# Query split of the next attention group, on VectorE, moved from one block of a group to three

## What is computed

```python
q = (_rmsnorm(cq, q_norm_g) @ w_uq).reshape(B, S, MLA_HEADS, MLA_NOPE_DIM + MLA_ROPE_DIM)
q = jnp.concatenate([q[..., :MLA_NOPE_DIM], _rope(q[..., MLA_NOPE_DIM:], cos, sin)], axis=-1)
...
def one(qblk):                       # 128 queries of every head against all 2048 keys
    s = jnp.einsum('bqhd,bkhd->bhqk', qblk, k, preferred_element_type=jnp.float32) * scale
    p = jax.nn.softmax(s, axis=-1).astype(v.dtype)
    return jnp.einsum('bhqk,bkhd->bqhd', p, v)
```

## Time and profile before

| | |
|---|---|
| median of 3 runs | 2358.72 us (2356.21 to 2360.28) |
| profiled execution | 2355.62 us |
| its span in the trace | 2353.8 us |
| attention (754.3 to 1377.0 us of the span), PE busy | 600.29 of 622.70 us |
| the same stretch, DVE, ACT, POOL busy | 462.20, 365.57, 203.97 us |
| granted TensorE clock there | 1.00 of full speed (2.4 GHz) |

### The profile page before, as it was taken

One profiled execution on the slowest core, in us unless ns is written; L12 is line 12 of the kernel. 1 busy time (PEld: TensorE's weight loads), 2 busy tenths in 40 slices (PEclk: granted clock), 3 DMA queues, 4 the chain that ended last, 5 costly groups with the idle time before them and its releaser, 6 DMA issues. The chain is left out here.

```text
span 2353.8 us, 34599 instructions
## 1 busy us (share of the span) xinstructions
PE 2256.6 (96%) x11426; PEld 1894.3 (80%) x11426; DVE 1404.0 (60%) x2146; ACT 1156.8 (49%) x2160; POOL 1025.7 (44%) x762
## 2 busy tenths in 40 slices
PE   5999998999998999999999989998999999999998
PEld 4888887989897778777777768887888888877886
DVE  7333336444445777767677751215999999983342
ACT  4555534222324655555555545556556565653432
POOL 6322222222223432323333132332989999982454
PEclk9999999999999999999999999999999999999999
DMA  7533323434343533434342224331111211253653
GB/s 298 179 134 134 134 76 139 152 127 151 127 145 118 150 105 98 107 94 116 85 119 82 90 104 143 118 123 42 44 59 41 68 54 43 74 177 114 174 161 107
DMA packets 196117, 271.15 MB, mean 115 GB/s; under 512 B 10532, under 2 KB 137764, under 8 KB 191398
## 3 DMA queue, kind: packets, MB, share of 16 engines
q1 hardware_dynamic: 191398, 261.43, 34.7%
q10 hardware_dynamic: 4608, 8.39, 1.0%
HBM read 183.27 MB, written 86.51 MB: 115 GB/s over the span
## 5 line engine op out<-in xcount | busy, mean ns | idle before, releaser
L2353 POOL TENSOR_TENSOR conv_g<-conv_g,product 128x1024 f32<-128x1024 f32 x160 | 384.9, 2408 | 34.3 <-ACT product L2402 24.6
L2500 DVE SCALAR_TENSOR_TENSOR ps_b<-u,cols,ps_b 128x1024 f32<-128x1024 f32 x304 | 391.7, 1288 | 9.2
L2616 PE MATMUL ps_a<-ho_hi,wp_lo 128*128 128x512 f32 x768 | 300.8, 392 | 6.8 <-DVE h_left L2556 6.8
L2617 PE MATMUL ps_a<-h_left,wp_hi 128*128 128x512 f32 x768 | 300.0, 391 | 0.0
L2618 PE MATMUL ps_a<-ho_hi,wp_hi 128*128 128x512 f32 x768 | 299.9, 391 | 0.0
L2402 ACT ACTIVATE product<-u,cols 128x1024 f32<-128x1024 f32 x160 | 183.3, 1151 | 170.0 <-POOL conv_g L2353 168.7
L1605 ACT ACTIVATE pt_hi<-ps_pt 128x512 fp32r<-128x512 f32 x256 | 154.4, 604 | 197.5 <-PE ps_pt L1801 197.3
L1716 DVE TENSOR_TENSOR pt_lo<-ps_pt,pt_hi 128x512 fp32r<-128x512 f32 x256 | 175.9, 688 | 119.7 <-ACT pt_hi L1605 116.9
L1660 POOL TENSOR_TENSOR v_lo<-v_st,v_hi 128x512 fp32r<-128x512 f32 x64 | 84.2, 1316 | 237.0 <-DVE v_hi L1692 237.0
L1706 DVE TENSOR_REDUCE mx<-ps_s 128x1 f32<-128x512 f32 x248 | 167.0, 684 | 21.3 <-PE ps_s L1793 20.3
L2616 PEld LDWEIGHTS ps_a<-ho_hi,wp_lo 128*128 128x128 f32 x768 | 145.0, 189 | 38.6 <-DVE h_left L2556 8.7
(11 more groups left out here) (449 smaller groups left out, 5629.0 us busy)
## 6 DMA issues: line engine op xcount, KB each, us to landing
scratch_ret_pack<-pack SPq DMA_DIRECT2D x14, 1280.0 KB, 5.4
pack<-scratch_ret_pack SPq DMA_DIRECT2D x14, 1280.0 KB, 7.0
k_st<-scratch_k_t SPq DMA_DIRECT2D x64, 256.0 KB, 3.5
v_st<-scratch_v SPq DMA_DIRECT2D x64, 256.0 KB, 3.7
ada<-in_ada_w_dram SPq DMA_DIRECT2D x16, 768.0 KB, 6.2
wp_raw<-in_od_w_in_dram SPq DMA_DIRECT2D x24, 512.0 KB, 4.1
xt<-in_x_dram SPq DMA_DIRECT2D x16, 512.0 KB, 6.1
ada<-in_ada_w_dram SPq DMA_DIRECT2D x8, 1024.0 KB, 8.8
```

The source lines that it names most:

```text
L2353: pool.tensor_tensor(half(conv_g, h), half(conv_g, h), product[adds(c, i, h) % 2][:], ALU.add).then_inc(added, 1)
L2500: dve.scalar_tensor_tensor(acc[h], units(c, k, h), params(c, k), acc[h], ALU.mult, ALU.add).then_inc(tap, 1)
L2616: pe.matmul(dst, lo[:, k, :], h_hi[:, k, t], start=k == 0, stop=False)
L2617: pe.matmul(dst, hi[:, k, :], h_lo[:, k, t], start=False, stop=False)
```

## The change

The three DVE instructions of `split_q` become three functions. `rot_high` (cast of `q_rot`, with its waits for the query load and for the group before) now stands at the end of block 0, `query_high` (cast of `q_hi`) at the end of block 1, `rot_low` (the low rotary half) at the end of block 2, each behind that block's `v_hi`. Nothing is added or removed on any engine.

```diff
-            def split_q(m, sl):
+            def rot_high(m, sl):
                 hold(dve, st, q_in, 48 * (m + 1))
                 if not (isinstance(m, int) and m < 2):
                     hold(dve, st, s_done, 16 * (m - 1))
                 dve.tensor_copy(q_rot[sl][:], qr_st[:]).then_inc(rot_hi, 1)
+
+            def query_high(m, sl):
                 dve.tensor_copy(q_hi[sl][:], q_st[:]).then_inc(qhi_done, 1)
+
+            def rot_low(m, sl):
                 hold(dve, st, rot_hi, m + 1)
                 dve.tensor_tensor(q_rot[sl][ROPE:P, :], qr_st[ROPE:P, :], q_rot[sl][ROPE:P, :].bitcast(F32),
                                   ALU.subtract).then_inc(rot_ready, 1)
...
-                    if score and not last(n, 1) and b == 1:
-                        split_q(n + 1, 1 - s)
+                    if score and not last(n, 1) and b < 3:
+                        (rot_high, query_high, rot_low)[b](n + 1, 1 - s)
```

## The result

The changed kernel took 2366.99 us (median of 7 runs, 2362.34 to 2373.38) beside 2359.08 for the kernel before on the same chip (2356.21 to 2360.56). The ratio is 1.0036, 95% interval 1.0021 to 1.0050: about 8 us slower, where 7 us faster had been forecast. Its profiled execution took 2366.68 us, span 2364.9, that is 11.1 us more span than before. Two executions took far longer than all others of their kernels (8030.22 us, one of 32 of the kernel before beside experiments 1 to 4, and 3648.95 us, one of six of experiment 6); the ratios leave them out.

A forecast was written before the change was run, and what follows sets the result against it. PE was taken as the bound, waiting for DVE in block 2. Block 2 -12.1, block 3 +3.4 and step 0 +1.9 gave -6.8 us, 2351.9 for the median; the range was to take in 2346.5 and 2357.5 but not 2366.2.

The forecast's parts named there:

- What bounds: PE busy 96%; in block 2 it waits for the left-over tile's `pt_lo`, held by DVE's list, not ACT.
- block 2: PE's wait at its second turn, steps 1 to 14, vanishes: 12.1 us gained.
- `q_hi` at 0.42: The cast of `q_hi`, moved ahead of POOL's `v_lo` in block 1, takes about 0.42 us instead of 1.50.
- `rot_high` in block 0 free: Its 0.42 us behind `v_hi` is hidden by DVE's 0.70 us idle before block 1: cost 0.
- Step 0: `rot_high` waits for the first query load ahead of block 1's maxima; PE restarts 1.9 us later in step 1.
- Block 3: `rot_low` in block 2 delays block 3's bias by 0.60 us, so the next step's scores wait: 3.4 us in sum.
- Four more are in block 0 of a new pass of the loop, which no edit touches: Four of PE's 20 low-part waits, in block 0 of a new loop pass, taken as unaffected.
- it goes 0.6 us later with some 10 us in hand: SP's query load, now waiting for `rot_low` at the end of block 2, goes 0.6 us later at no cost.
- The rivals: Block 3's delay misses PE: 2349.0, chance 0.20; POOL first: 2366.2, 0.08; gain falls short: 2358.0, 0.17.
- rival 2: In block 2 POOL's `v_lo` starts first, `rot_low` costs 1.08 us more: +7.5 us, 2366.2; chance 0.08.

The follow-up runs named there:

- experiment 1: The changed kernel, but in step 0 the three instructions stay together in block 1 as before: 2363.09 us (ratio 1.0016).
- experiment 2: The changed kernel, but `rot_low` goes to block 1 behind `query_high`: 2356.36 us (ratio 0.9988).
- experiment 3: The changed kernel, but SP issues the 768 KB modulation load in block 1 instead of block 0: 2356.21 us (ratio 0.9989).
- experiment 4: The kernel before, with only the modulation load moved from block 0 to block 1: 2357.77 us (ratio 0.9994).
- experiment 6: The changed kernel with step 0 split as before and the modulation load issued in block 1: 2350.60 us (ratio 0.9959).
- experiment 7: The kernel before with `split_q` whole in block 1 ahead of the `v_hi` cast, and the modulation load in block 1: 2344.01 us (ratio 0.9932).
- experiment 8: The changed kernel with `rot_low` in block 0 behind `rot_high`, step 0 as before, modulation load in block 1: 2344.55 us (ratio 0.9935).
- experiment 11: The kernel before with `split_q` whole in block 1 ahead of the `v_hi` cast, modulation load where it was: 2347.91 us (ratio 0.9948).
- experiment 5: The kernel before, but SP also waits for block 3's multiply-add before the query loads, DVE's list untouched: 2366.70 us (ratio 1.0033).

## Why the prediction was wrong
- **What bounds, and block 2: right.** PE was held by DVE's list behind `split_q`; the wait is gone, 12.4 us for 12.1. (Step 1 had been put at 0.57 from its wait; cut like the others it is 0.48.)
- **`q_hi` at 0.42: right** (412 to 420 ns in all 15), and by the port, as experiment 2 shows for its neighbour.
- **`rot_high` in block 0 free: right** in all steps but 0.
- **Step 0: mechanism right, size off.** PE's restart was forecast 1.9 us later; it came 3.5 us later, and 1.6 us of lower clock followed, which the forecast had no term for and which came in other traces without the edit too. The chain was right as far as the wait for the load (4.8 forecast, 4.73), but it priced the subtraction at 0.69, not at POOL-first's 1.78, and the multiply at 1.01.
- **Block 3: mechanism right, size off.** 3.4 forecast, 4.9 in the trace. In the even steps PE waits 0.38 to 0.40 (0.31 forecast), in the odd ones 0.24 (0.04). From the start of `v_hi` to that of the gates it is now 0.45 + 0.72 = 1.17 us for 0.34, a shift of 0.83; I took 0.60 of a range that ended at 0.72.
- **The step that failed: "Four more are in block 0 of a new pass of the loop, which no edit touches", and "it goes 0.6 us later with some 10 us in hand".** I asked of SP's delayed loads only whether their data would come in time. I didn't ask what else uses DMA just then. The waits in block 0 had been read and put aside, though DVE's rows there show it idle for 2.7 us without an engine to blame. The runs showed in its place that the loads, issued 0.3 to 0.6 us nearer to the return, lengthen DVE's idle time from 2.7 to 3.1 us to 3.3 to 5.4, and that this costs PE 10.6 us in block 0: 6.0 of longer waits, and nearly all the rest by PE at the lower clock. The forecast put it at 0. Without that term the sum of the trace's own pieces is -1.5; with it, +9.1.
- **The rivals.** That the time came out near rival 2's 2366.2 is chance: its mechanism did not occur in block 2 beyond step 0: `rot_low` takes 0.69 in 14 of 15 cases. The slowdown had a place that none of the rivals named.

What stays open: why so small a shift delays the transfer by so much. A load issued 0.3 to 0.6 us later against the return lengthened DVE's idle time by 0.5 to 2.7 us, and unevenly. In part the loss on PE is larger than that because its clock fell behind the longest waits. The changed kernel's runs also spread over 11 us (2362.3 to 2373.4), those of experiment 3 over 7. Which of the transfers in flight the fetch stood behind, the trace does not tell; moving the 768 KB away was enough. No run moved the values' or the query's load alone.

## What to carry to other kernels
Ask of every step that is moved what it does to the time at which the DMA queue issues, and what else wants DMA then; a hardware loop's return is such a consumer, and large loads should not be in flight over it. Before a burst on VectorE is spread over an iteration, look at what makes it long: here 1.1 of its 3 us were GpSimd holding the port, and putting the burst ahead of the cast that sets GpSimd going was worth more than spreading it, and cost nothing elsewhere. An idle time without a plausible releaser at the same place of each pass is a term of the sum, not noise. And a new wait of PE can cost more than its length: look at the granted clock behind it.

## What the runs showed of the hardware
- A return of this loop costs VectorE 2.3 to 2.6 us idle with no load in flight (experiments 3, 4, 6, 7 and 8), 2.4 to 3.1 with the 768 KB load issued 4.1 to 4.3 us ahead of it (before, experiments 2 and 11), and 3.0 to 5.4 with it issued 3.3 to 3.7 us ahead (after, experiments 1 and 5). An 8 KB instruction transfer starts behind the return, 0.3 to 0.4 us with no load in flight and up to 3.4 us after the change, and VectorE resumes 2.0 to 2.3 us behind that start. Written out, the same code shows no such idle time, though instruction transfers go on.
- Of a VectorE subtraction with two SBUF inputs and a GpSimd subtraction, the later one waits: 1.55 to 1.79 us for 0.69 where GpSimd began 0.06 to 0.3 us ahead, 0.69 where VectorE did (`v_lo` then takes up to 1.80 for 1.29).
- TensorE's granted clock was 0.50 (1.2 GHz) from 969.9 to 973.2 and from 1205.4 to 1212.2 after the change, at and behind waits of PE of 3.05 and 3.12 us, and 1.00 behind those of 0.99 and 2.03 us at the other two returns.
